# First mixer's output projection as seven half-width products per chunk, with the borrowed ring places filled later

## The chip, the cores and the metric

The kernel runs on one core of a Trainium2 chip. The metric is the device time of one execution in microseconds (us), lower is better; the time before is the median of three runs.

Engines, as the profile names them: PE (TensorE matmul), PEld (its weight load), DVE (VectorE), ACT (ScalarE), POOL (GpSimd), SP (SyncE, which here only issues DMAs; SPq in the rows). Matmuls write PSUM, which has 8 banks of 128 x 512 f32 words.

## The reference, cut to what matters

Two networks run one after the other on 256 tokens of width 1024. The first has two layers, and layer 0 works on two streams: the latent tokens `x` and the context `ctx`, 256 tokens each. Its mixer is `conv_mixers`:

```python
def conv_mixers(u, w_in, conv_a, conv_b, conv_b_bias, ln_g, ln_b, w_out):
    p = u @ w_in
    gate_out, gate_in, val, glu_a, glu_g = jnp.split(p, ...)
    y_a = gate_out * depthwise_conv(gate_in * val, conv_a)          # 512 channels
    z = depthwise_conv(glu_a * jax.nn.sigmoid(glu_g), conv_b) + conv_b_bias
    y_b = jax.nn.silu(layer_norm(z, ln_g, ln_b))                    # 512 channels
    return jnp.concatenate([y_a, y_b], axis=-1) @ w_out             # 1024 x 1024
```

The result of both streams is added to the residual, `h + mod[2] * y`, and then each stream goes through an expert layer: 16 experts, each takes its 32 best tokens, with `w_gate`, `w_up` and `w_down` of 1024 x 1024 (4 MB each in f32). A second mixer (attention and a long convolution) and a second expert layer follow, and then the second network.

## The kernel before, in words

Everything is f32. Activations lie with channels on the 128 partitions. `H` ("hidden" in the rows) is the residual, 2 streams x 8 blocks of 128 channels x 256 tokens; `ab.Y` ("ab_y") holds the mixer's 1024 channels as 8 blocks (0 to 3 are `y_a`, 4 to 7 are `y_b`) of 512 columns, the 256 tokens of one stream and then the other's.

**The weight stream.** All large weights come as one stream of 644 chunks of 1 MB (1024 KB), issued by SP in a fixed order (`sync_program`, the `dma_start` at line 832). A chunk fills a slot; two slots are a place. There are 7 places of the ring's own (`ring` in the rows). For the first half of the first expert layer, two more are borrowed (`M.more_ring[0]`): one made of `ring_filter_freq` and `ring_pads`, one of `ring_z` and `ring_filter`. `Ring.__init__` (from line 718) gives each pair of chunks the place that has waited longest, and `come` says from which pair on the borrowed places take part. The chunk of an earlier pair in the same place must have been used up by PE (`chunk_free`, raised by `ring.free`), and SP waits for that in order: a transfer whose wait isn't over holds up all transfers behind it. Counting pairs of chunks from the first pair of the expert weights as pair 0, `come` is pair 1 here, and SP waits before pair 1 for the last `y_b` block (line 819), since the borrowed room holds mixer data until then. Some pairs go as one transfer of 2 MB, some as two of 1 MB (`transfers`, line 391).

The pairs around the change, in order, with the place that each takes before: output weights `out_ab` 0 and 1 (`ring0`), one modulation pair (`ring1`), `out_ab` 2 and 3 (`ring2`), three modulation pairs (`ring3` to `ring5`), then pair 0 (`ring6`), pairs 1 and 2 (borrowed), pair 3 (`ring0`), 4 (`ring1`), 5 (`ring2`), 6 to 8 (`ring3` to `ring5`), 9 (`ring6`), 10 and 11 (borrowed), 12 (`ring0`) and so on. Pairs 0 to 95 are the expert weights of the first expert layer, pairs 98 to 105 belong to the second mixer.

**The output projection.** `out_ab` c is the 1024 x 256 slice of `w_out` that makes channel blocks 2c and 2c+1. `project_back` (line 1000) makes each block with 8 matmuls of 128 x 128 weights against 512 columns of `ab.Y` (both streams at once) into one bank. The trace counts two instructions for each f32 matmul. DVE's `back` (line 2493) adds each block to `H` with two instructions (line 2498). In the middle of a block PE does `route` (line 968) for the block before: the router's share of that block and four transposes per block for the expert layer's token-major copy (`U2T`). Block 7's `route` follows after the last block; it also sums the squares that ACT (line 2008) and POOL (line 3381) make of every finished block. Then `moe(0)` begins with the first modulation product after it, then the top-32 selection on DVE, and then the expert products, which use the pairs in order.

## Time and profile before

| | us |
|---|---|
| median of 3 runs (2549.83 to 2551.3) | 2550.35 |
| the profiled execution's own time | 2549.89 |
| its span, first to last instruction | 2548.5 |
| PE busy in the span | 2457.0 (96%) |
| DVE busy | 1257.3 (49%) |
| ACT busy | 436.4 (17%) |
| DMA, mean over the span | 280 GB/s |

The profile is of one execution. Its rows give times from the first instruction on. A busy PE is not a PE at its peak, and the shares are means over stages that have different limits: the page's 40 slices show the DMA engines full in some and half idle in others.

### The profile page before, as it was taken

The numbers are of one execution on the slowest core, as the hardware profiler recorded it, in microseconds if no ns is written. First come the engines' busy times: TensorE is split into PE (matmuls) and PEld (weight loads), VectorE is DVE, ScalarE is ACT, GpSimd is POOL, SyncE is SP. The second block draws the span as 40 slices with busy tenths as digits, with TensorE's granted clock in tenths as the row PEclk, the third lists the DMA queues.
The fourth block names the chain that finished last, engine by engine and source line by source line (L and its number), as shares of the span: only waits on it lengthen the run. The fifth ranks groups of instructions, "written<-read, shape, count | busy, mean of one in ns | idle before, by whom it ended". The sixth has DMA issues, their size and how long they took to land.

```text
span 2548.5 us, 29532 instructions
## 1 busy us (share of the span) xinstructions
PE 2457.0 (96%) x12286; PEld 1553.7 (61%) x12286; DVE 1257.3 (49%) x2175; ACT 436.4 (17%) x1099; POOL 179.5 (7%) x126
## 2 busy tenths in 40 slices
PE   9999999889999999987889999999999999999999
PEld 5344443424578753332348857888866875888884
DVE  4981321212176621110117667665776775673775
ACT  2111100101123210000001002541101101560110
POOL 0011000000000000000000011440001003250000
PEclk9999999999999999999999999999999999999999
DMA  9854899999984499999999863415674974423671
GB/s 394 332 231 181 355 425 427 426 428 428 423 345 165 169 377 427 427 427 427 427 421 341 259 222 149 150 67 210 215 227 154 257 227 154 169 106 135 221 225 39
DMA packets 193904, 712.88 MB, mean 280 GB/s; under 512 B 117284, under 2 KB 121892, under 8 KB 128364
## 3 DMA queue, kind: packets, MB, share of 16 engines
q1 hardware_dynamic: 92592, 682.66, 67.2%
q10 hardware_dynamic: 101180, 28.35, 5.3%
q8 instruction: 97, 1.59, 0.3%
q14 instruction: 35, 0.29, 0.0%
HBM read 698.36 MB, written 12.60 MB: 279 GB/s over the span
## 4 chain that ended last, share of the span: by engine, by line
PE 77%; DMA 16%; DVE 5%; ACT 1%; issue 0%; POOL 0%; SPq 0%; DVEq 0%; another core or an unknown queue 0%; POOLq 0%
PE bank L855 75%; DMA ring<-in_stream 8%; DMA ring_high<-in_stream 4%; DMA ring_low<-in_stream 4%; PE bank L858 2%; DVE hidden L2731 1%; DVE ab_z L2561 1%; DMA hidden_turned<-normed 1%; DVE moe_results L2756 0%; DVE small L3300 0%; DVE hidden L3297 0%; DVE small L3303 0%; POOL ab_ln_sum L3426 0%; ACT hidden L2376 0%; DVE ring L3067 0%
## 5 line engine op out<-in xcount | busy, mean ns | idle before, releaser
L855 PE MATMUL bank<-ring,gates 128*128 128x256 f32 (+1 forms) x1760 | 433.6, 391 | 3.5 <-DVE ring L3067 2.4
L855 PE MATMUL bank<-ring,moe_chosen 128*64 128x512 f32 (+1 forms) x2304 | 391.7, 491 | 33.1 <-DMA ring<-in_stream 32.8
L855 PEld LDWEIGHTS bank<-ring,gates 128*128 128x128 f32 x1760 | 333.6, 190 | 71.1 <-issue 23.0
L855 PE MATMUL bank<-ring,normed 128*128 128x256 f32 x1448 | 339.5, 380 | 1.4 <-DMA ring<-in_stream 1.4
L855 PEld LDWEIGHTS bank<-ring,moe_chosen 128*64 128x64 f32 x2304 | 147.8, 137 | 248.9 <-issue 197.1
L855 PEld LDWEIGHTS bank<-ring,normed 128*128 128x128 f32 x1448 | 273.2, 190 | 40.7 <-issue 2.3
L855 PE MATMUL bank<-normed,ring 128*128 128x256 f32 (+2 forms) x1152 | 289.4, 406 | 2.4 <-DVE normed L2542 1.5
L855 PEld LDWEIGHTS bank<-normed,ring 128*128 128x128 f32 x1152 | 189.4, 190 | 98.7 <-issue 84.2
L855 PE MATMUL bank<-ring,ffn_hidden 128*128 128x512 f32 x352 | 170.6, 592 | 0.0
L855 PE MATMUL bank<-ring,moe_turned 128*64 128x512 f32 x576 | 128.8, 595 | 17.5 <-DMA ring<-in_stream 14.3
L2747 DVE TENSOR_TENSOR moe_silu<-bank,moe_silu 128x512 f32<-128x512 f32 x32 | 22.1, 692 | 249.4 <-PE bank L855 249.4
L2756 DVE COPY moe_results<-bank 32x512 f32<-32x512 f32 x36 | 24.8, 690 | 243.1 <-PE bank L855 242.7
L3067 DVE TENSOR_TENSOR ring<-ring,ring 128x1024 f32<-128x1024 f32 x117 | 142.2, 1215 | 1.6
L855 PEld LDWEIGHTS bank<-ring,ffn_hidden 128*128 128x128 f32 x352 | 66.9, 190 | 82.5 <-issue 75.6
L2267 ACT ACTIVATE gates<-gates,small 128x256 f32<-128x256 f32 x88 | 44.4, 508 | 411.6 <-DVE gates L3080 222.2
L855 PEld LDWEIGHTS bank<-ring,moe_turned 128*64 128x64 f32 x576 | 41.1, 137 | 100.9 <-issue 84.3
L2081 ACT COPY moe_results<-bank 32x512 f32<-32x512 f32 x36 | 20.7, 575 | 466.7 <-PE bank L855 466.4
L2561 DVE SCALAR_TENSOR_TENSOR ab_z<-ab_pad_b,vectors,ab_z 128x512 f32<-128x512 f32 x120 | 90.2, 752 | 4.3
L3067 DVE TENSOR_TENSOR ring<-ring 128x1024 f32<-128x1024 f32 x71 | 85.8, 1209 | 0.0
L855 PE MATMUL bank<-ring,hidden 128*128 128x512 f32 x168 | 84.5, 592 | 0.0
L3147 DVE TENSOR_TENSOR ring<-ring 128x512 f32<-128x512 f32 x88 | 62.2, 706 | 38.2 <-PE bank L855 38.2
L3442 POOL TENSOR_TENSOR na_bias<-na_bias,na_mask 128x512 f32<-128x512 f32 x16 | 21.4, 1374 | 782.0 <-PE bank L855 782.0
(448 smaller groups left out, 2720.4 us busy)
## 6 DMA issues: line engine op xcount, KB each, us to landing
ring<-in_stream SPq DMA_DIRECT2D x318, 1024.0 KB, 7.3
ring<-in_stream SPq DMA_DIRECT2D x115, 2048.0 KB, 30.5
ring_low<-in_stream SPq DMA_DIRECT2D x7, 2048.0 KB, 43.7
ring_far<-in_stream SPq DMA_DIRECT2D x7, 2048.0 KB, 45.3
ring_high<-in_stream SPq DMA_DIRECT2D x6, 2048.0 KB, 45.1
hidden_turned<-normed ACTq DMA_DIRECT2D x44, 256.0 KB, 7.3
ffn_hidden<-hidden_turned ACTq DMA_DIRECT2D x44, 256.0 KB, 7.3
hidden<-in_stream SPq DMA_DIRECT2D x9, 1024.0 KB, 31.0
```

The costliest lines, as they stand in the source:

```text
L855: return nc.tensor.matmul(o, lhsT, rhs, start=start, stop=stop, skip_group_check=True)
L858: return nc.tensor.transpose(o, x, ident[0:x.shape[0], 0:x.shape[0]])
L2081: ins = nc.scalar.copy(m.YG[CAP * e:CAP * e + CAP, i, 0:512], bank[4][CAP * i:CAP * i + CAP, :])
L2267: nc.scalar.activation(y.sg[:, t, :], (y.C2 if t else y.C1)[:, 0, :], ACT.Silu, scale=y.rinv_t[:, t:t + 1]).then_inc(*done.up((tag, l, "si ...
L2561: ins = v.scalar_tensor_tensor(out=z_j, in0=ab.PB[:, :, k:k + T], scalar=tap("conv_b", k, j), in1=z_j, op0=ALU.mult, op1=ALU.add)
L2731: v.scalar_tensor_tensor(out=H[:, s, n, :], in0=bank[5 + n % 3][:, T * i:T * i + T], scalar=M.MOD[:, l, 5, n, s:s + 1], in1=H[:, s, n, :], ...
L2747: v.tensor_tensor(m.SG, bank[1][:, :], m.SG, ALU.mult).then_inc(*done.up((tag, "hidden", g, e)))
L2756: ins = v.tensor_copy(m.YG[CAP * e:CAP * e + CAP, i, 512:1024], bank[4][64 + CAP * i:64 + CAP * i + CAP, :])
L3067: v.tensor_tensor(tw[:, i], a, b, ALU.subtract).then_inc(*done.up((tag, l, "t", c, i)))
L3147: v.tensor_tensor(to[:, i], a, b, ALU.subtract).then_inc(*done.up((tag, l, "dt", c, i)))
L3442: nc.gpsimd.tensor_tensor(part, part, mask, ALU.add).then_inc(*done.up(("na_bias", l, t) if h == NA_H - 2 else None))
```

## The change

The four output chunks are each computed with the seven block products of a 2 x 2 scheme in place of eight. For chunk c the weights are cut into four blocks: rows `gated` (k 0 to 3, the `y_a` half) and `normed` (k 4 to 7), columns 2c and 2c+1. The tokens are cut likewise: `gated` and `normed` rows by stream 0 and stream 1. Each product is 4 matmuls of 128 x 128 weights against 256 columns.

- DVE makes, per chunk, four sums of weight blocks (`out_weight_sums`, three of them into new tiles and one over the chunk itself in its ring slot), and once four sums of token blocks (`out_token_sums`, 128 x 1024 each).
- PE's `out_group` runs the seven products into banks 4 (`first`), 2, 5 and 1; `route` for the two blocks of the chunk before stands behind the third and the fourth product; `route` for blocks 6 and 7 both stand behind the last group.
- ACT copies bank 4 into `ab.first`; DVE's `out_sums` puts the products together with four additions and adds the four pieces to `H` (line 2597 in the changed kernel).
- The tiles of sums lie in the room of the two borrowed places. So `come` moves from pair 1 to pair 3, and SP's wait before it is now for `("ab", "back", 7)`, DVE's very last addition of the projection.

```diff
+    four_blocks = lambda name, at, n, width: put(name, arena + 4 * at, n, 4, width)
+    pads, filters = -(-low // 8) * 8, -(-high // 8) * 8
+    here, there = four_blocks("ab_token_sums", filters, 2, T), four_blocks("ab_token_sums_2", pads, 2, T)
+    ab.TS = [here[:, 0], here[:, 1], there[:, 0], there[:, 1]]
...
-BACK_BANKS = {"ab": (4, 5, 1, 2), "cd": (2, 3, 4, 5)}
+AB_OUT_GROUPS = KB // 2
+AB_FIRST_BANK, AB_PRODUCTS = 4, (2, 5, 1)
...
-        come = self.come = [at("expert", 0, 0, 0, 0) + 1, at("expert", 1, 0, 0, 0) + 3]
+        come = self.come = [at("expert", 0, 0, 0, 0) + 3, at("expert", 1, 0, 0, 0) + 3]
...
         if i == 2 * ring.come[0]:
 
-            sp.wait_ge(*S.scalar.at(("y_b", JB - 1)))
+            sp.wait_ge(*S.vector.at(("ab", "back", 2 * AB_OUT_GROUPS - 1)))
...
+        pe.wait_ge(*ring.landed(name))
+        pe.wait_ge(*A.at(("ab", "first", c - 1) if c else ("y_b", JB - 1)))
+        product(first[:, 0:T], block(0, normed), tokens(normed, 0)).then_inc(*done.up(("ab", "first", c)))
+        if c:
+            pe.wait_ge(*V.at(("ab", "z", c - 1)))
+        product(z[:, T:2 * T], weights(0), summed(0))
+        for j in range(0 if c else JB):
+            pe.wait_ge(*V.at(("y_a", j)))
+        product(x[:, 0:T], block(0, gated), tokens(gated, 0))
+        if c:
+            route(0, "ab", 2 * c - 2)
+            pe.wait_ge(*V.at(("ab", "w", c - 1)))
+        product(w[:, T:2 * T], weights(3), tokens(gated, 1))
+        if c:
+            route(0, "ab", 2 * c - 1)
+        product(x[:, T:2 * T], weights(1), summed(1)).then_inc(*done.up(("ab", "x", c)))
+        product(z[:, 0:T], weights(2), summed(2)).then_inc(*done.up(("ab", "z", c)))
+        product(w[:, 0:T], block(1, gated), summed(3)).then_inc(*ring.free(name))
...
-        project_back(0, "ab", "out_ab", ab.Y, 512, (*range(JB, KB), *range(JB)))
+        for c in range(AB_OUT_GROUPS):
+            out_group(c)
+            if c == 1:
+
+                pe.wait_ge(*V.at(("moe0", "shift")))
+                ada_part(1, 1, 0)
+        route(0, "ab", KB - 2)
+        route(0, "ab", KB - 1)
...
         for k in range(KB):
+            if l == 0 and k in (0, 2, 4):
+                for c in range(2) if k == 0 else (k // 2 + 1,):
+                    first(c)
...
+        dve.wait_ge(*TE.at(("ab", "x", c)))
+        dve.wait_ge(*done.now())
+        v.tensor_tensor(two(y0), two(x[:, :]), wide(ab.first, 2), ALU.add).then_inc(*done.up(("ab", "x", c)))
+        dve.wait_ge(*done.now())
+        added(0, 2 * c, y0[:, 0:T]).then_inc(*done.up())
+        dve.wait_ge(*TE.at(("ab", "z", c)))
+        v.tensor_tensor(two(y1), two(z[:, :]), wide(y0[:, T:2 * T], 2), ALU.add).then_inc(*done.up())
+        dve.wait_ge(*done.now())
+        v.tensor_tensor(y0[:, T:2 * T], y1[:, 0:T], z[:, T:2 * T], ALU.add).then_inc(*done.up(("ab", "z", c)))
+        dve.wait_ge(*S.chunk.at(("out_ab", c)))
+        dve.wait_ge(*done.now())
+        v.tensor_tensor(y1, y1, w[:, :], ALU.add).then_inc(*done.up(("ab", "w", c)))
...
         gated(AB_OUT_ORDER[0])
+        out_weight_sums(0)
         invert("ln_root", ab.rinv)
         for j in range(JB):
             v.tensor_tensor(ab.Z[:, j, :], ab.Z[:, j, :], ab.rinv, ALU.mult).then_inc(*done.up(("whitened", j)))
-        for j in AB_OUT_ORDER[1:]:
+        for j in AB_OUT_ORDER[1:-1]:
             gated(j)
+        out_token_sums((0,))
+        gated(AB_OUT_ORDER[-1])
+        out_token_sums((1, 2, 3))
         ada(*AB_PAIRS[len(AB_STEPS) - 1])
         fold(0, 1)
         fold(1, 0)
         dve.wait_ge(*done.now())
         router_weights(0)
-        back("ab", "out_ab", 0, (0, 1))
+        out_weight_sums(1)
+        out_back()
```

SP's transfers from pair 0 on. Before, in the order of issue (128x4096 is a whole pair, 128x2048 one chunk or one piece of a borrowed place):

```order
L832 DMA ring6_55<-in_stream 128x4096
L832 DMA ring_filter_freq_137<-in_stream 128x2048
L832 DMA ring_pads_138<-in_stream 128x2048
L832 DMA ring_z_139<-in_stream 128x2048
L832 DMA ring_filter_140<-in_stream 128x2048
L832 DMA ring0_49<-in_stream 128x4096
L832 DMA ring1_50<-in_stream 128x2048 x2
L832 DMA ring2_51<-in_stream 128x2048 x2
```

The same place in the changed kernel:

```order
L842 DMA ring6_55<-in_stream 128x4096
L842 DMA ring0_49<-in_stream 128x4096
L842 DMA ring1_50<-in_stream 128x4096
L842 DMA ring_filter_freq_137<-in_stream 128x2048
L842 DMA ring_pads_138<-in_stream 128x2048
L842 DMA ring_z_139<-in_stream 128x2048
L842 DMA ring_filter_140<-in_stream 128x2048
L842 DMA ring2_51<-in_stream 128x2048 x2
```

Pairs 1 and 2 now go to `ring0` and `ring1`, which come free when the second output chunk and the modulation pair are used up, and the borrowed places get pairs 3 and 4, ahead of pair 5 in `ring2`.

PE from the start of the projection. Before, to the end of block 2 (`small` is the modulation's condition; `kept` holds the identity and ones):

```order
L855 MATMUL bank4<-ab_y_82,ring0_49 128x512 x8
L855 MATMUL bank5<-ab_y_82,ring0_49 128x512 x5
L855 MATMUL bank3<-moe0_router_91,kept_59 128x32 x8
L858 MATMUL bank6<-kept_59,hidden_56 128x128 x4
L855 MATMUL bank5<-ab_y_82,ring0_49 128x512 x3
L855 MATMUL bank1<-ab_y_82,ring0_49 128x512 x5
L855 MATMUL bank0<-hidden_56,moe0_router_91 32x256 x4
L858 MATMUL bank7<-kept_59,hidden_56 128x128 x4
L855 MATMUL bank1<-ab_y_82,ring0_49 128x512 x3
```

Now, the first group and the first products of the second:

```order
L865 MATMUL bank4<-ab_y_82,ring0_49 128x256 x4
L865 MATMUL bank5<-ab_token_sums_144,ab_weight_sums_146 128x256 x4
L865 MATMUL bank2<-ab_y_82,ring0_49 128x256 x4
L865 MATMUL bank1<-ab_y_82,ab_weight_sums_146 128x256 x4
L865 MATMUL bank2<-ab_token_sums_144,ab_weight_sums_146 128x256 x4
L865 MATMUL bank5<-ab_token_sums_2_145,ring0_49 128x256 x4
L865 MATMUL bank1<-ab_token_sums_2_145,ring0_49 128x256 x4
L865 MATMUL bank4<-ab_y_82,ring0_49 128x256 x4
L865 MATMUL bank5<-ab_token_sums_144,ab_weight_sums_2_147 128x256 x4
L865 MATMUL bank2<-ab_y_82,ring0_49 128x256 x4
L865 MATMUL bank3<-moe0_router_91,kept_59 128x32 x8
```

Two blocks of 8 x 512 columns became 28 x 256 columns, and the first `route` moved from the middle of block 1 to behind the third product of the second group.

DVE behind one chunk. Before, the two blocks of chunk 0 and the copy of the router's shift:

```order
L2498 SCALAR_TENSOR_TENSOR hidden_56<-bank4,modulation_62,hidden_56 128x256 x2
L2498 SCALAR_TENSOR_TENSOR hidden_56<-bank5,modulation_62,hidden_56 128x256 x2
L2504 COPY moe0_shift_92<-bank3 128x32
```

Now, for the same chunk:

```order
L2608 TENSOR_TENSOR ab_sums_149<-bank2,ab_first_148 128x512
L2597 SCALAR_TENSOR_TENSOR hidden_56<-ab_sums_149,modulation_62,hidden_56 128x256
L2612 TENSOR_TENSOR ab_sums_2_150<-bank5,ab_sums_149 128x512
L2614 TENSOR_TENSOR ab_sums_149<-ab_sums_2_150,bank5 128x256
L2617 TENSOR_TENSOR ab_sums_2_150<-ab_sums_2_150,bank1 128x512
L2597 SCALAR_TENSOR_TENSOR hidden_56<-ab_sums_2_150,modulation_62,hidden_56 128x256 x2
L2597 SCALAR_TENSOR_TENSOR hidden_56<-ab_sums_149,modulation_62,hidden_56 128x256
L2584 TENSOR_TENSOR ab_weight_sums_146<-ring2_51 128x512
```

Three of the four pieces of a chunk, for both of its blocks, now reach `H` only after the chunk's seventh product, and the weight sums of the chunk after the next stand between two chunks.

## Rows read from the trace of the kernel before

**Rows 1.** The page: transfer rate in 40 slices of the span (64 us each).
```profile
GB/s 394 332 231 181 355 425 427 426 428 428 423 345 165 169 377 427 427 427 427 427 421 341 259 222 149 150 67 210 215 227 154 257 227 154 169 106 135 221 225 39
```

**Rows 2.** Windows: stretch, length, busy us (x instructions) of each engine, PEclk, DMA share, GB/s.
```profile
195.00:263.00 68.00, 67.79 (x249) 32.24 (x251) 10.50 (x36) 11.47 (x20) 7.62 (x6) 1.00 0.48 184
330.00:437.00 107.00, 104.50 (x516) 43.32 (x514) 26.02 (x58) 12.34 (x24) 0.00 (x0) 1.00 1.01 426
437.00:740.00 303.00, 275.17 (x1725) 136.43 (x1722) 80.05 (x187) 43.15 (x105) 5.08 (x4) 1.00 1.01 425
```

**Rows 3.** Timeline of PE: start, us, what, [idle before it <- what ended it].
```profile
442.85 3.65 PE L855 MATMUL bank<-ring,moe_chosen 128*64 128x512 f32 x16 [1.34 <-DMA ring<-in_stream]
...
728.97 10.63 PE L855 MATMUL bank<-ring,normed 128*128 128x256 f32 x48 [1.42 <-DMA ring<-in_stream]
```

**Rows 4.** Timeline of SP, single issues: start, us, what.
```profile
195.10 0.33 SPq L832 DMA_DIRECT2D ring<-in_stream  x1
...
197.20 0.47 SPq L832 DMA_DIRECT2D ring_filter<-in_stream  x1
...
226.34 0.33 SPq L832 DMA_DIRECT2D ring<-in_stream  x1
...
259.06 0.33 SPq L832 DMA_DIRECT2D ring<-in_stream  x1
...
264.57 0.33 SPq L832 DMA_DIRECT2D ring<-in_stream  x1
...
277.50 0.33 SPq L832 DMA_DIRECT2D ring<-in_stream  x1
...
312.51 0.33 SPq L832 DMA_DIRECT2D ring<-in_stream  x1
```

**Rows 5.** DMA issues in windows of one issue: us to landing, issues at 197.20, 259.06, 312.51, 434.5.
```profile
ring_filter<-in_stream SPq DMA_DIRECT2D x1, 1024.0 KB, 15.5
...
ring<-in_stream SPq DMA_DIRECT2D x1, 1024.0 KB, 4.8
...
ring<-in_stream SPq DMA_DIRECT2D x1, 2048.0 KB, 16.7
...
ring_filter_freq<-in_stream SPq DMA_DIRECT2D x1, 1024.0 KB, 35.2
```

**Rows 6.** Timeline of PE, the projection and what follows.
```profile
194.91 11.32 PE L855 MATMUL bank<-ab_y,ring 128*128 128x512 f32 x26
...
226.24 1.92 PE L855 MATMUL bank<-ring,small 128*32 128x512 f32 x16
...
258.86 0.95 PE L855 MATMUL bank<-kept,ab_sigmoid 128*128 128x1 f32 x8
...
262.58 1.92 PE L855 MATMUL bank<-ring,small 128*32 128x512 f32 x16
```

**Rows 7.** Windows of PE alone: 16 matmul instructions of 512 columns, and 16 of 256.
```profile
240.96:247.83 6.87, 6.87 (x18) 1.00 0.41 150
771.83:775.29 3.46, 3.46 (x18) 1.00 0.83 348
```

**Rows 8.** Groups by line: busy us, mean ns of one | idle before.
```profile
L855 PEld LDWEIGHTS bank<-ring,normed 128*128 128x128 f32 x1448 | 273.2, 190 | 40.7 <-issue 2.3 <-DMA ring<-in_stream 1.9 <-DVE normed L3022 0.6
L3067 DVE TENSOR_TENSOR ring<-ring,ring 128x1024 f32<-128x1024 f32 x117 | 142.2, 1215 | 1.6
```

**Rows 9.** Timeline of DVE before and in the projection.
```profile
182.10 3.35 DVE L2439 RECIPROCAL ab_rinv<-ab_rinv 128x512 f32<-128x512 f32 x1 [5.35 <-ACT ab_rinv L1885]
...
195.11 0.69 DVE L2598 TENSOR_TENSOR ab_y<-ab_y,bank 128x512 f32<-128x512 f32 x1 [5.93 <-PE bank L855]
...
197.16 0.28 DVE L2630 TENSOR_TENSOR moe_router<-vectors,modulation 128x128 f32<-128x128 f32 x1
...
259.06 0.88 DVE L2498 SCALAR_TENSOR_TENSOR hidden<-bank,modulation,hidden 128x256 f32<-128x256 f32 x2 [6.43 <-PE bank L855]
```

**Rows 10.** Timeline of POOL, the sum of the squares of block 6.
```profile
253.38 1.27 POOL L3381 TENSOR_TENSOR ab_sigmoid<-ab_sigmoid,ab_squares 128x512 f32<-128x512 f32 x1 [6.75 <-ACT ab_squares L2008]
```

More of the change, by code:

```diff
@@ new lines, in out_token_sums @@
+    def out_token_sums(which):
+        ab = M.ab
+        tokens = lambda ks, s: ab.Y[:, ks, T * s:T * s + T]
+        gated, normed = slice(0, JB), slice(JB, KB)
+        terms = ((tokens(normed, 1), tokens(normed, 0)), (tokens(gated, 1), ab.TS[0]), (tokens(gated, 1), tokens(normed, 1)), (tokens(gated, 0), ab.TS[1]))
+        for i in which:
+            dve.wait_ge(*(done.now() if i else A.at(("y_b", JB - 1))))
+            v.tensor_tensor(ab.TS[i], *terms[i], ALU.subtract).then_inc(*done.up(("ab", "t", i)))
@@ L2506, in mixer_ab, with out_back @@
+    def out_back():
+        for c in range(AB_OUT_GROUPS):
+            if c == 1:
+                dve.wait_ge(*TE.at(("moe0", "shift")))
+                v.tensor_copy(M.moe[0].shift, bank[SHIFT_BANK[0]][:, 0:NS * NE]).then_inc(*done.up(("moe0", "shift")))
+            out_sums(c)
+            if c + 2 < AB_OUT_GROUPS:
+                out_weight_sums(c + 2)
     def mixer_ab():
```

61 lines of the change are left out of this document (55 added, 6 removed).

## The prediction

> **What bounds the kernel now.** Read the rate of the DMA engines over the whole span first [rows 1]. From the sixth slice to the eleventh (319 to 701 us) it stands near 426 GB/s, and nowhere above 428: that is the stream of expert weights. In slices 3 and 4, around the change, it falls to 231 and 181, and in 13 and 14, the second mixer, to 165 and 169. Then read the stretches around the change [rows 2]: in the output projection (195 to 263) PE is busy and the DMA engines are at 0.48; from 330 to 437 both are full, at 426 GB/s; from 437 to 740 the DMA engines are full and PE has 28 us of gaps. The gaps end on landings: I show the one at 442.85 (pair 40), and the last, for the second mixer's first weights, at 728.97 [rows 3]. So PE is ahead of the stream up to 437, and from there to 729 it does each piece when it lands. What PE gains before 437 is only a longer wait after it. The end of the kernel is moved by what moves the landings, and those are gated by when SP can issue.
>
> The issues say where the stream has holes [rows 4]. Pairs 0 to 2 go out from 195.10 on; pair 3 at 226.34, when `out_ab` 1 is used up; the second half of pair 5 at 259.06, pair 6 at 264.57. Between them the queue runs dry. Pair 17 is issued at 312.51 and lands 16.7 us later, at 329.2 [rows 5]; from there to pair 102 one transfer follows the other. I take the landing of pair 17 as the gauge: what the change does to it, it does to the end.
>
> **The change on PE.** A block of 16 instructions with 512 columns takes 6.87 us, a product's 8 with 256 columns half of 3.46, 1.73 us; the granted clock is 1.00 (2.4 GHz) in both [rows 7]. The second is measured in the other mixer, with the same shape and the same kind of sums, so I take it as it is. Eight blocks are 55.0 us, 28 products 48.4: 6.6 us less. The projection now runs from 194.91 to 258.86 [rows 6]: 63.95 us, of which 55.0 are blocks, 1.9 the modulation part, 7.1 seven `route` calls. One that has transposes alone (for block 6) moves behind the last product; I estimate it at 0.4, below the mean of 1.0, as it lacks the router's part. The last product then ends at 194.91 + 48.4 + 1.9 + 6.7 = 251.9, if nothing waits.
>
> Does something wait? The first product needs the last `y_b`. That is what SP waits for between pairs 0 and 1, and as the issues of 195.10 and 197.20 stand 2.1 us apart with three others between them [rows 4], it was over by then. The third needs the last gated block, at 195.80 [rows 9], and comes at 194.9 + 2 x 1.73 = 198.4. The first chunk's weight sums, four additions of 512 elements at half of the 1.22 us that 1024 take [rows 8], some 2.5 us, fall into the 5.35 us in which DVE waits for the root [rows 9]. The first token sum falls into the 5.93 us before 195.11. The other three are 1.22 us each [rows 8]: 195.80 to 199.4; the fifth product, the first that needs one, comes at 201.8. Then come what stood there before (195.80 to 197.4, 1.7 us) and the second chunk's weight sums (2.5): DVE is free at 203.7, and the fifth product, for which it waits next, ends at 203.8. PE's next need is bank 5 at 194.91 + 8 x 1.73 = 208.75; DVE has it free 0.7 + 0.4 us behind the sixth product (205.5), at 206.7. Slack 2.0 us here, and more in later groups, where DVE has some 6 us of work in 14. So no wait, at cost nothing; were DVE later by more than 2.0, PE would be later by the rest.
>
> **The change behind the last product.** Before, DVE starts 0.2 us behind the last matmul and needs 0.88 [rows 6, 9]. Now it adds bank 1 (0.69) and then three pieces (0.88 + 0.45): 251.9 + 0.2 + 0.7 + 1.3 = 254.1. That is the wait of SP before pair 3. PE's own tail: block 6 is on `H` only at 253.2, ACT squares it (0.6), POOL needs 1.27 [rows 10], and the sum of squares that began at 258.86 now begins at 255.1. What followed it took 3.7 us up to 262.58 [rows 6]. The expert layer starts on PE at about 258.8, 3.8 us earlier.
>
> **The change on the stream.** Queued behind SP's waiting instruction are pairs 3, 4 and all after them. Pairs 1 and 2 wait for `out_ab` 1 and the modulation pair, used up at about 222 (194.9, 14 products, the first two `route` calls) and 224, and are there by 237; PE, which is done with pair 0 near 273.7, wants them after that. At 254.1 pairs 3, 4 and 5 go out in one burst, as all they wait for is over; pair 6 joins at about 260.8 (before 264.57, less 3.8), pairs 7 and 8 within 4 us, pair 9 when pair 0 is used, near 273.7 (277.50 before [rows 4]), when pairs 6 to 8 are still to come. From there each pair is issued 3.8 us earlier than before, while its turn comes later, so I see no hole.
>
> A pair is 2.097 MB; at 426 GB/s [rows 2] that is 4.92 us. The start of a burst costs more: pairs 0 to 2 were issued from 195.10, the last piece landed at 197.20 + 15.5 = 212.7 [rows 4, 5], so 17.6 for 14.8, a surcharge of 2.8. Pair 17 is the fifteenth from pair 3: 254.1 + 2.8 + 15 x 4.92 = 330.7. Before 329.2. The change of the end is +1.5 us. The saving of the seven products is in it: without it SP would be released at 260.7 and the sum would be +8.1. Put otherwise, the later filling of two pairs costs 9.8 us of stream and gets back what the earlier end and the holes of before (12 pairs from 264.57 to 329.2 are 64.6 us, 59.0 of them transfer) leave.
>
> Bounds. From below, the chain ends 0.5 us sooner and the surcharge is that of a lone chunk: 4.8 to landing [rows 5], 2.46 of it transfer, so 2.3: +0.5. From above, the holes that pairs 6 to 17 have beyond a surcharge, 64.6 - 59.0 - 2.8 = 2.8, come again: +4.3. I take +1.5, since the queue is deeper in every place where those holes were.
>
> Later the ring's places are shifted too: the borrowed places leave at pair 48 having held pairs 39 and 40, not 46 and 47, so pairs 48 to 54 wait for pairs 41 to 47, two further than before. That is 9.8 us of lead, of 35.2 at pair 46 [rows 5]; 25 are left. Pairs 99 and 100 also wait for two later ones, with over 20 us of lead left. Cost nothing, covered by the queue.
>
> The profiled execution took 2549.89 with a span of 2548.5; the same sum gives 2551.4. The median of the runs shown is 2550.35, 0.46 above it, so 2551.9.
>
> **A rule against it.** A window of 16 matmul instructions with 256 columns holds 16 weight loads of 190 ns [rows 7, 8] and takes 16 x 216: the loads lie under the matmuls. The Trainium skill, "TensorE: Matmul & The Clock Gate", section "The mechanism", says that a weight load overlaps a running matmul only when it goes to another row group of the array, and these all use all rows. By that rule loads would be exposed. Here the trace disagrees, with 216 ns an instruction. A rival below holds what it would cost.
>
> **Rivals.**
> - PE sets the end after all, and its earlier start is kept: -3.8 us, 2546.5; were the tail hidden as well, the whole 6.6, 2543.7. For it: PE is 96% busy. Against: 28 us of gaps between 437 and 740, ended by landings [rows 2, 3]. 0.08, a half of it with the whole 6.6.
> - DVE holds PE between groups, and it ends slower. The place is bank 5 before the second product of group 1, the point a DVE lateness of 2.0 us. All of these sums read every other half row of a tile. If they ran at half speed, 3.7 + 2.5 = 6.2 us more, less 2.0, PE and SP's release come 4.2 later: +5.7, 2556.1. For it: DVE goes without a pause from 195 to 207. Against: additions of ring halves cut the same way take 1.22 for 1024 [rows 8]. 0.15.
> - The weight loads are not covered at 256 columns: 96 more loads of 190 ns, +18.2 on the projection and so on SP's release: +19.7, 2570. The page above would have it so. Against: rows 7. 0.02.
>
> **How the numbers follow.** Forecast 0.75, its own range +0.5 to +4.3, 2550.9 to 2554.7. About 0.2% (5.1 us) is what a measurement of this kernel can tell from no change. Faster than that: the half of the first rival and a little for what I overlook, 0.05. Slower: most of the second, the third, and a thin end of the forecast (holes and a little lateness together), 0.17. The rest, 0.78, within. For 8 in 10 the range goes from 2547, short of the first rival's value, to 2557, past the second's.
>
> **What would show it.** In the profile after: products of 1.73 us, the last one ending near 252; SP's issue into `ring_filter_freq` at about 254 (before 195.5); the DMA engines idle between 235 and 256 and then full with no gap; pair 17 landing near 330.7; PE's first wait for a landing before 437, its gaps up to 740 some 4 to 6 us larger; the first weights of the second mixer at about 730.4 (before 728.9). I am wrong if pair 17 lands before 329 or after 334, if PE waits for DVE in groups 1 to 3, or if the shift at 729 is not the one at pair 17.

## The result

The kernel after takes 2554.70 us (median of 20 runs), the kernel before beside it 2551.29 (20 runs). By the medians that is 3.4 us slower. The ratio of the runs is 1.0018, 95% interval 1.0012 to 1.0024, so 4.6 us with 3.1 and 6.1 as its bounds: it goes with the means, and a few long runs of the kernel after (up to 2566.31) lift its mean to 2555.94. The profiled execution took 2553.35 with a span of 2552.0, 3.46 more than that of before. The prediction said 2551.9, with 0.78 for a change within 0.2% (it is, narrowly), 2550.9 to 2554.7 for the mechanism that it named (the median is at the upper end), and +1.5 us where +3.4 came. So the mechanism has to be shown, and the 1.9 us that it was short be found.

**The projection.** The timeline of PE in the kernel after (start, us, what, idle time before it and what ended it), in the place of [rows 6] and [rows 7]:

```profile
207.45 1.89 PE L865 MATMUL bank<-ab_y,ring 128*128 128x256 f32 x8
209.18 1.89 PE L865 MATMUL bank<-ab_token_sums,ab_weight_sums 128*128 128x256 f32 x8
...
248.84 3.62 PE L865 MATMUL bank<-ab_token_sums,ring 128*128 128x256 f32 x16
253.76 0.66 PE L868 MATMUL bank<-kept,hidden 128*128 128x128 f32 x4 [1.30 <-DVE hidden L2597]
255.77 1.05 PE L865 MATMUL bank<-kept,ab_sigmoid 128*128 128x1 f32 x8 [1.35 <-POOL ab_sigmoid L3514]
256.75 0.78 PE L865 MATMUL bank<-hidden,moe_router 128*32 128x256 f32 x8
257.45 1.87 PE L865 MATMUL bank<-kept,ab_squares 128*128 128x1 f32 x8
...
261.06 3.33 PE L865 MATMUL bank<-ring,small 128*32 128x512 f32 x16
```

From one product's start to the next it is 1.73 us (207.45 to 209.18), as reckoned, and the last ends at 248.84 + 3.62 = 252.5. The first starts at 195.37 and not at 194.91, which is 0.46 of the 0.6 between 252.5 and the 251.9 of the prediction. Windows of the kernel after show that PE never waits for DVE within the groups: 67.60 - 64.95 = 2.65 us of gaps in the first row are the 1.30 and the 1.35 above. And they show what I had not thought of, in the last column but two, the granted clock:

```profile
core 0: us, PE busy (x) PEld busy (x) DVE busy (x) ACT busy (x) POOL busy (x), PEclk, DMA share, GB/s
195.40:263.00 67.60, 64.95 (x353) 52.44 (x355) 33.71 (x71) 13.61 (x26) 8.17 (x6) 0.96 0.35 137
235.00:254.00 19.00, 17.70 (x92) 14.72 (x91) 8.02 (x15) 2.75 (x6) 2.54 (x2) 1.00 0.00 1
252.00:256.00 4.00, 1.35 (x9) 0.70 (x8) 2.24 (x5) 2.25 (x3) 1.27 (x1) 1.00 0.16 31
256.00:258.00 2.00, 2.00 (x19) 1.44 (x18) 0.00 (x0) 1.29 (x5) 0.00 (x0) 0.78 0.93 340
258.00:260.00 2.00, 2.00 (x11) 2.00 (x11) 0.18 (x1) 1.05 (x3) 0.00 (x0) 0.50 0.99 418
...
262.00:264.00 2.00, 2.00 (x16) 0.31 (x8) 0.30 (x2) 0.09 (x1) 0.00 (x0) 0.51 1.00 422
264.00:266.00 2.00, 2.00 (x22) 0.57 (x22) 1.18 (x4) 0.00 (x0) 0.00 (x0) 1.00 1.03 426
330.00:437.00 107.00, 102.95 (x506) 42.46 (x504) 26.02 (x58) 12.32 (x24) 0.00 (x0) 1.00 1.01 425
437.00:740.00 303.00, 273.81 (x1715) 134.02 (x1712) 76.67 (x184) 42.94 (x103) 5.08 (x4) 1.00 1.01 426
```

After the two gaps the clock falls to 0.50 (1.2 GHz) until about 264. The modulation part that took 1.92 us in [rows 6] takes 3.33. So TensorE begins that part 1.5 us earlier than before, not 3.8, and by its end it has only 0.1 us left of its gain.

**The stream.** Single issues of SP in the kernel after, for [rows 4]: pair 0, pair 3, the second half of pair 5, pair 6, pair 9, pair 17.

```profile
195.56 0.33 SPq L842 DMA_DIRECT2D ring<-in_stream  x1
...
254.52 0.33 SPq L842 DMA_DIRECT2D ring_filter_freq<-in_stream  x1
...
257.30 0.47 SPq L842 DMA_DIRECT2D ring<-in_stream  x1
...
264.46 0.33 SPq L842 DMA_DIRECT2D ring<-in_stream  x1
...
277.38 0.33 SPq L842 DMA_DIRECT2D ring<-in_stream  x1
...
312.39 0.33 SPq L842 DMA_DIRECT2D ring<-in_stream  x1
```

The times to landing of the second half of pair 5 and of pair 17 in the kernel after, the latter for the 16.7 of [rows 5]:

```profile
ring<-in_stream SPq DMA_DIRECT2D x1, 1024.0 KB, 15.7
...
ring<-in_stream SPq DMA_DIRECT2D x1, 2048.0 KB, 20.1
```

Pair 17 lands at 312.39 + 20.1 = 332.5, before at 329.2. The same shift stands 400 us later at the first weights of the second mixer. This is PE's row there, before at 728.97 [rows 3]:

```profile
732.42 10.63 PE L865 MATMUL bank<-ring,normed 128*128 128x256 f32 x48 [1.41 <-DMA ring<-in_stream]
```

It is 3.45 us later, and the span is 3.5 us longer. Between these two executions, nothing is won or lost from pair 17 to the end.

### The profile page after: what moved, and what is told of

It reads as the page before. It is cut to its first block, busy times and chain, and to the rows that moved or that the text cites. A ratio compares the mean times of both kernels' runs of the same rounds, so it can differ in the third digit from the quotient of the medians.

```text
span 2552.0 us, 29776 instructions
## 1 busy us (share of the span) xinstructions
PE 2455.0 (96%) x12382; PEld 1573.1 (62%) x12382; DVE 1285.0 (50%) x2211; ACT 437.2 (17%) x1103; POOL 180.8 (7%) x126
## 4 chain that ended last, share of the span: by engine, by line
PE 77%; DMA 17%; DVE 4%; ACT 1%; issue 0%; POOL 0%; SPq 0%; another core or an unknown queue 0%; DVEq 0%; POOLq 0%
PE bank L865 75%; DMA ring<-in_stream 9%; DMA ring_high<-in_stream 4%; DMA ring_low<-in_stream 3%; PE bank L868 2%; DVE hidden L2864 1%; DVE ab_z L2689 1%; DMA hidden_turned<-normed 1%; DVE moe_results L2889 0%; SPq L842 0%; POOL ab_ln_sum L3559 0%; DVE ring L3200 0%; DVE cd_y L2502 0%; DVE moe_turned L2885 0%; DVE small L3433 0%
## 5 line engine op out<-in xcount | busy, mean ns | idle before, releaser
L865 PE MATMUL bank<-ring,moe_chosen 128*64 128x512 f32 (+1 forms) x2352 | 400.8, 491 | 30.5 <-DMA ring<-in_stream 30.5
L865 PEld LDWEIGHTS bank<-ring,normed 128*128 128x128 f32 x1448 | 273.0, 190 | 42.3 <-issue 3.1
```

What stands on the lines that cost most here:

```text
L865: return nc.tensor.matmul(o, lhsT, rhs, start=start, stop=stop, skip_group_check=True)
```

## The experiments

All of them against the kernel before, which ran beside them (median 2551.60 in the first four, 2552.06 in the next four, 2551.79 in the last three). The gauge columns come from each profiled execution as they did above, one for each kernel. The medians of before differ by up to 0.8 us from one group of experiments to the next, so a difference of less than about 1 us between the medians of two groups tells nothing.

```
kernel                 pair 3 asked  pair 17 lands  2nd mixer on PE  span    median   ratio (95%)
before                 226.34 (own)  329.2          728.97           2548.5  2551.29
after                  254.52        332.5          732.42           2552.0  2554.70  1.0018 (1.0012-1.0024)
ring_only              260.59        338.4          738.21           2558.2  2559.51  1.0035 (1.0022-1.0048)
tail_warm              254.67        332.8          732.65           2551.3  2553.70  1.0012 (1.0003-1.0021)
early_release          253.67        332.1          731.94           2551.5  2552.80  1.0004 (0.9995-1.0013)
parts_moved            in own place  333.5          733.37           2556.2  2556.98  1.0021 (1.0012-1.0030)
sums_later             254.14        332.4          732.27           2554.5  2554.42  1.0009 (1.0000-1.0018)
light_before                                        703.10           2523.2  2525.22  0.9896 (0.9882-0.9909)
light_after                                         704.08           2524.3  2524.91  0.9894 (0.9880-0.9907)
light_warm                                          699.88           2520.3  2521.20  0.9879 (0.9865-0.9892)
part_alone             in own place  331.9          731.69           2551.5  2552.37  1.0001 (0.9992-1.0009)
before_part                          330.6          730.35           2550.8  2552.53  1.0003 (0.9994-1.0012)
one_part               in own place  327.3          727.66           2547.6  2549.81  0.9989 (0.9980-0.9998)
```

**ring_only: the ring part without the new projection.**

```diff
--- before
-        come = self.come = [at("expert", 0, 0, 0, 0) + 1, ...
+        come = self.come = [at("expert", 0, 0, 0, 0) + 3, ...
-            sp.wait_ge(*S.scalar.at(("y_b", JB - 1)))
+            sp.wait_ge(*S.vector.at(("ab", "back", KB - 1)))
```

> The kernel before with its old output projection, and of the change only the ring part: the borrowed places are filled from pair 3 on instead of pair 1, behind the last addition of the old projection. In the kernel after, pair 3 was asked for at 254.5 us and pair 17 landed 3.3 us later than in the kernel before. Theory (the stream decides: the time is what the last landings make it, and they move with the request of pair 3): the old projection's last addition ends near 260, so the request moves some 5.5 us later than in the kernel after, pair 17 lands at about 338 (329.2 before, 332.5 after), and the run is 7 to 9 us slower than before. Rival (TensorE decides: its own start into the expert layer sets the end): the old projection ends as it did, so the time stays within 1 us of before.

Measured: 2559.51, 7.9 us over before. SP's issue of pair 3 and the time to landing of pair 17, in the trace of this kernel:

```profile
260.59 0.33 SPq L832 DMA_DIRECT2D ring_filter_freq<-in_stream  x1
...
313.13 0.33 SPq L832 DMA_DIRECT2D ring<-in_stream  x1
```

```profile
ring<-in_stream SPq DMA_DIRECT2D x1, 2048.0 KB, 25.3
```

The request of pair 3 is 6.07 us later than in the kernel after, and pair 17 lands 5.9 us later (338.4): one for one. The second mixer follows by 5.8 and the span by 6.2; between the medians it is 4.8. The whole change thus splits. The later filling costs 9.2 us at pair 17, the shorter projection gives 5.9 back.

**tail_warm: TensorE kept busy in the two gaps.**

```diff
--- after
+        def hold_clock(n):
+            for i in range(n):
+                mm(bank[AB_FIRST_BANK][:, 0:T], ones, M.kept[:, 0:T], True, True)
+
+        pe.wait_ge(*A.at(("ab", "first", AB_OUT_GROUPS - 1)))
+        hold_clock(3)
         route(0, "ab", KB - 2)
+        hold_clock(4)
         route(0, "ab", KB - 1)
```

> The kernel after with seven more 128x256 products whose sums nobody reads, three ahead of the routing of block 6 and four ahead of that of block 7, in the two gaps of 1.30 and 1.35 us in which TensorE waited. Both theories: the granted clock stays at 1.0 between 256 and 266 us, where it was 0.50 from 257 to 264, and TensorE comes into the expert layer at about 258, 3 us earlier. Theory (the stream decides): the request of pair 3 is VectorE's and does not move, so the landing of pair 17 moves by less than 1 us and the median by 0.5 us at most. Rival (the lost clock is what ate the gain): 2 to 3 us faster than the kernel after, so at or below the kernel before.

Windows of this kernel show a clock that stays, and its timeline of PE the modulation parts (one, and then two in one row) at full speed again, 1.6 and 3.0 us earlier than in the kernel after (261.06 and 264.64):

```profile
256.00:258.00 2.00, 2.00 (x22) 1.55 (x20) 0.00 (x0) 1.30 (x5) 0.00 (x0) 1.00 0.85 299
258.00:260.00 2.00, 2.00 (x22) 1.53 (x25) 0.86 (x5) 1.89 (x4) 0.00 (x0) 1.00 1.05 442
...
262.00:264.00 2.00, 2.00 (x24) 0.65 (x20) 1.86 (x7) 0.00 (x0) 0.00 (x0) 1.00 1.07 442
```

```profile
259.50 1.92 PE L865 MATMUL bank<-ring,small 128*32 128x512 f32 x16
...
261.68 3.64 PE L865 MATMUL bank<-ring,small 128*32 128x512 f32 x32
```

Pair 17 lands at 332.8 and the second mixer begins at 732.65, 0.2 later than in the kernel after: three microseconds of TensorE changed nothing there. The median is 1.0 below that of the kernel after, more than the 0.5 that I allowed; the two ratios' intervals overlap (1.0003 to 1.0021 and 1.0012 to 1.0024). The trace has no such gain before 732; in the profiled execution 0.9 us arise behind it (2551.3 - 732.65 = 1818.7, against 1819.6 in the kernel after), where the edit changes nothing. I count the rival's 2 to 3 us as refuted by the landings and the 1.0 as open.

**early_release: pair 3 released by TensorE's last product.**

```diff
--- after
-    ab.first = put("ab_first", arena + 4 * (end1 + TT * 2 * T + 3 * 4 * P), T)
+    ab.first = put("ab_first", arena + 4 * (high + SLOT), T)
-            sp.wait_ge(*S.vector.at(("ab", "back", 2 * AB_OUT_GROUPS - 1)))
+            sp.wait_ge(*S.chunk.at(("out_ab", AB_OUT_GROUPS - 1)))
-        y0, y1 = ab.both
+        y0, y1 = (ab.both if c < AB_OUT_GROUPS - 1 else (ab.Y[:, JB - 1, :], ab.both[1]))
```

> The kernel after, with the last group's intermediate sums put outside the borrowed ring places, so that the transfer of pair 3 waits for the last read of the output weights by TensorE's products and not for VectorE's last additions. The request of pair 3 moves from 254.5 to about 252.3. Theory (the stream decides): the landing of pair 17 moves from 332.5 to about 330.5 and the run is 1.5 to 2.5 us faster than the kernel after, slightly above the kernel before. Rival (the stream is held by the ring places of pairs 6 to 17, which TensorE's clock and start set): no more than 0.3 us.

Measured: 2552.80, 1.9 below the kernel after. In the profiled execution the projection began 1.2 us later than in that of the kernel after (pair 0 asked at 196.74), so the request of pair 3 must be read from there: 253.67 - 196.74 = 56.9 us, against 254.52 - 195.56 = 59.0. It is 2.0 earlier, and pair 17, read the same way, 1.6.

**parts_moved: all of the second modulation's pairs ahead.**

```diff
--- after
         if c == 1:
-            ada_quarter(1, 1, 0)
-    for q in range(1, KB // 2):
-        ada_quarter(1, 1, q)
+            for q in range(KB // 2):
+                ada_quarter(1, 1, q)
...
-        come = self.come = [at("expert", 0, 0, 0, 0) + 3, ...
+        come = self.come = [at("expert", 0, 0, 0, 0) + 6, ...
...
-                ada_part(1, 1, 0)
+                for q in range(KB // 2):
+                    ada_part(1, 1, q)
...
-        modulation = (lambda q: ada_part(1, 1, q + 1)) if l == 0 else ...
+        modulation = (lambda q: kept_warm(4)) if l == 0 else ...
```

> The kernel after, with all four pairs of the second layer's modulation streamed and multiplied ahead of the last projection chunks (between chunk 1 and chunk 2) and none between the routing and the first experts; the borrowed places are then filled from the third expert pair on as before, counted from the new order. TensorE gets 5.8 us of work earlier and loses it behind the projection, and the three ring places of those pairs come free some 20 to 30 us earlier. Theory (the stream decides, and it stood idle between 236 and 254 us for want of places): about half of that idle time is filled, and the run is 2 to 7 us faster than the kernel after. Rival (the stream's idle time is only moved, since the projection's end and with it the borrowed places' release comes 5.8 us later): within 1.5 us of the kernel after, or slower by up to 3.

Measured: 2556.98, 2.3 slower than the kernel after. The theory's number was wrong, the rival's right (up to 3 slower). At pair 17 only 1.0 of it is seen (333.5), and 0.7 of that is a later start, so the step from pair 9 to the 2.3 is not shown; where the profiled execution loses more stands at the end of the section on the prediction. Windows of this kernel show where the stream stands still now:

```profile
278.00:282.00 4.00, 4.00 (x32) 3.27 (x32) 1.37 (x6) 1.50 (x4) 0.00 (x0) 1.00 0.00 0
282.00:286.00 4.00, 4.00 (x25) 2.08 (x22) 0.39 (x2) 0.00 (x0) 0.00 (x0) 1.00 0.41 152
```

Three more pairs land by 252, but pair 9 needs a place that the use of pair 0 frees, and TensorE, 5.5 us later, comes to that at 282.9 (277.4 after). The queue has run dry by 278.7. I had looked at the places before the borrowed ones alone. A single pair more, in place of three, is tried in part_alone and one_part.

**sums_later: VectorE's sums away from GpSimd's.** The four sums of the first chunk move behind the first token sum.

```diff
--- after
         gated(AB_OUT_ORDER[0])
-        out_weight_sums(0)
         invert("ln_root", ab.rinv)
...
         out_token_sums((0,))
+        out_weight_sums(0)
```

> The kernel after with the first chunk's four weight sums moved on VectorE from ahead of the reciprocal at 182.5 us to behind the token sum at 189.6 us, where VectorE has 4.7 us of idle time; they no longer run beside GpSimd's three additions at 175.6 us. Theory (the two engines slow each other, and GpSimd's additions hold TensorE's product of ones): those three additions take 4.4 us instead of 4.93, each sum takes 0.7 us instead of up to 1.75, the projection starts 0.4 to 0.5 us earlier, and the run is about 0.5 us faster, which the interval can hardly tell. Rival (the 0.5 us are a scatter from run to run): the additions stay at 4.9 us.

The sums and GpSimd's additions, first in the trace of the kernel after:

```profile
176.60 1.16 DVE L2584 TENSOR_TENSOR ab_weight_sums<-ring 128x512 f32<-128x512 f32 x1
177.79 1.64 DVE L2584 TENSOR_TENSOR ab_weight_sums<-ab_weight_sums,ring 128x512 f32<-128x512 f32 x1
179.36 1.75 DVE L2584 TENSOR_TENSOR ring<-ring 128x512 f32<-128x512 f32 x1
181.03 0.68 DVE L2584 TENSOR_TENSOR ab_weight_sums<-ring,ab_weight_sums 128x512 f32<-128x512 f32 x1
```

```profile
175.62 4.93 POOL L3559 TENSOR_TENSOR ab_ln_sum<-ab_ln_sum,ab_squares 128x512 f32<-128x512 f32 x3 [8.49 <-ACT ab_squares L2041]
```

and then with the sums later:

```profile
190.39 0.68 DVE L2584 TENSOR_TENSOR ab_weight_sums<-ring 128x512 f32<-128x512 f32 x1
191.11 0.69 DVE L2584 TENSOR_TENSOR ab_weight_sums<-ab_weight_sums,ring 128x512 f32<-128x512 f32 x1
```

```profile
175.77 4.41 POOL L3559 TENSOR_TENSOR ab_ln_sum<-ab_ln_sum,ab_squares 128x512 f32<-128x512 f32 x3 [8.50 <-ACT ab_squares L2041]
```

Apart, the additions take 4.41 and each sum 0.68; beside each other 4.93 and up to 1.75. The product of ones behind them comes 0.4 us earlier (at 180.32, before at 180.70) and with it the projection. The Trainium skill, "SBUF — State Buffer", section "Who interferes with whom", says that a DVE instruction with both inputs in SBUF contends with a GpSimd instruction that reads SBUF; the trace agrees in that, with the numbers above. Of VectorE's two-port modes it also says that whoever issues first has the shared ports for the whole instruction and the other is blocked. Here, with additions that both read two tiles of SBUF, both are longer while they overlap (4.93 for 4.41 on one side, 1.16 + 1.64 + 1.75 for 3 x 0.68 on the other), so over a string of instructions each engine loses some time. The median, 0.3 below that of the kernel after, can't tell 0.5 from nothing.

**light_before and light_after: the stream out of the way.** In both, the transfers of the first expert layer are halved from pair 6 on.

```diff
+            if name[:2] == ("expert", 0) and i // 2 >= ring.come[0] + 3:      # + 5 on the kernel before
+                to, src = to[:, 0:SLOT * chunks // 2], src[:, 0:SLOT * chunks // 2]
             nc.sync.dma_start(to, src).then_inc(*ring.arrival(i).up(i if last else None))
```

> The kernel before, but from pair 6 of the first expert layer on only the first half of each transfer's columns is fetched (that layer's weights are stale beyond it, so the output is another one); every wait stays. It is the base for the next run. The stream should stop bounding the first expert layer: the expert layer of 460 us becomes shorter by what TensorE waited for, so 20 to 100 us in all.

> The kernel after with the same halved transfers. Read against the kernel before with halved transfers, not against the full ones. Theory (with full transfers the change costs what the late request of pair 3 costs the stream; TensorE itself comes to pair 0 only 0.1 us earlier, as its gain in the projection is lost to the halved clock): with the stream out of the way the 3.3 us are gone and the two differ by 0.5 us at most, either way. Rival (the change loses time on TensorE or VectorE as well, in the expert layer): after remains 2 us or more slower. A second rival (the projection's gain of some 4 us is real and only hidden by the stream): after is 3 us or more faster.

Windows, first of light_before, then of light_after. The stream is at 236 to 245 GB/s, and PE is busy for 248 of 253 us where it was busy for 227 to 229 with full transfers:

```profile
437.00:690.00 253.00, 247.99 (x1536) 119.15 (x1534) 60.70 (x144) 32.51 (x77) 3.79 (x3) 1.00 0.71 245
```

```profile
437.00:690.00 253.00, 247.99 (x1524) 118.44 (x1522) 60.11 (x142) 32.16 (x76) 3.79 (x3) 1.00 0.69 236
```

Before and after take 2525.22 and 2524.91 (4 runs each): the 3.4 us are gone. What was lost was lost in the stream, and TensorE brings nothing of the projection's 6.6 us with it, as expected from the 0.1 us above. (In the profiled executions light_after is 1.1 us longer; its projection began 1.6 us later, pair 0 being asked for at 196.56 and 194.98. The section on the prediction shows that most of these 1.6 come from near 20 us, where the edit has no part.)

**light_warm: the same with the clock held.** The edit of tail_warm on light_after.

> The kernel after with the halved transfers and with the seven products that hold the clock in the two gaps ahead of routing 6 and routing 7. Read against the kernel after with halved transfers (2524.91 us). Theory (the halved clock between 257 and 264 us costs TensorE 3 us, and this shows in the time as soon as the stream does not set it): TensorE comes to pair 0 at about 275 instead of 278, and the run is 2 to 3.5 us faster. Rival (something else than TensorE and the stream sets the expert layer, VectorE's or ScalarE's part in it): no more than 0.7 us.

PE comes to pair 0 at 272.18 (276.37 in light_after, 275.40 in light_before), to the second mixer at 699.88 (704.08, 703.10); the 275 and 278 of the expectation were both too late. The first of these rows, in light_after and then in light_warm:

```profile
276.37 3.65 PE L867 MATMUL bank<-ring,moe_chosen 128*64 128x512 f32 x16
```

```profile
272.18 3.65 PE L867 MATMUL bank<-ring,moe_chosen 128*64 128x512 f32 x16
```

The median is 3.7 us below light_after, just above the range of 2 to 3.5, and 4.0 below light_before. In the two profiled executions PE moves by 4.2, of which 1.1 lies in the start of the projection (pair 0 asked at 195.45 and 196.56) and 3.1 in the clock. With the stream out of the way, the clock's 3 us show in the time; this is the very edit that moved no landing with full transfers.

**part_alone and before_part: one modulation pair more ahead, on either kernel.**

```diff
         if c == 1:
             ada_quarter(1, 1, 0)
-    for q in range(1, KB // 2):
+            ada_quarter(1, 1, 1)
+    for q in range(2, KB // 2):
...
-        come = self.come = [at("expert", 0, 0, 0, 0) + 3, ...      # on before: + 1
+        come = self.come = [at("expert", 0, 0, 0, 0) + 4, ...      # on before: + 0
...
                 ada_part(1, 1, 0)
+                ada_part(1, 1, 1)
...
-        modulation = (lambda q: ada_part(1, 1, q + 1)) if l == 0 else ...
+        modulation = (lambda q: ada_part(1, 1, q + 1) if q else kept_warm(2)) if l == 0 else ...
```

> The kernel after with one edit: two modulation pairs instead of one behind chunk 1, so that four expert pairs fit ahead of the borrowed places. No products that hold the clock, no early release, the weight sums as in the kernel after. The four edits together made 4.9 us. Theory (the extra pair's transfer of about 5 us falls into the stream's idle time and 1.9 us of it are paid back, since TensorE and with it the release of the borrowed places comes 1.9 us later): 2.5 to 4 us faster than the kernel after, within 1 us of the kernel before; pair 17 lands at about 329.3. Rival (without the held clock the use of pair 0 comes too late for pair 9, as where all four were moved): less than 1 us faster than the kernel after.

> The kernel before with the same one edit: two modulation pairs instead of one behind chunk 1. The borrowed places are asked for behind the extra pair as early as before, near 195 us, by the first expert pair now. Theory (before has no backlog of transfers behind the old projection: pair 6 waits for a ring place that TensorE frees at 264.5 us and the queue is empty then, so TensorE's 1.9 us earlier work only delays it): no gain; pair 17 lands at 329 to 331 and the run is 0 to 2 us slower than before. Rival (an extra pair in the stream's idle time is worth 3 us in either kernel, so the faster version above owes nothing to the change): 2 to 4 us faster than before.

(`kept_warm(n)` makes n products that nobody reads.)

part_alone: 2552.37, 2.3 below the kernel after, just under the range. The gauge does not bear this out: pair 17 lands at 315.27 + 16.6 = 331.9, not at 329.3, so 0.6 earlier than in the kernel after, or 1.3 with the start taken out, which is 0.7 later (pair 0 asked at 196.22); its borrowed places are asked for at 256.90, and the clock is at 0.50 from 260 to 268 in its windows. before_part: 2552.53, 0.7 above before, pair 17 at 330.6, 1.4 later than in before. The rival is refuted. The stream does not stand on a backlog here: in before it moves 133 GB/s from 256 to 264, and windows of before_part show it waiting for places, with a clock that falls here too (0.50 from 264 to 266):

```profile
266.00:268.00 2.00, 2.00 (x16) 0.71 (x19) 1.11 (x5) 0.10 (x1) 0.00 (x0) 0.78 0.65 279
268.00:270.00 2.00, 2.00 (x24) 0.60 (x20) 1.86 (x7) 0.00 (x0) 0.00 (x0) 1.00 0.06 16
```

So the extra pair gained at the gauge in the kernel after, where six pairs are asked for between 254.5 and 268.8, and not in the kernel before. That the backlog makes the difference fits these rows; no run varies it by itself, and the fallen clock of before_part may have a part in its 1.4.

**one_part: the four edits together.** early_release, tail_warm, sums_later and part_alone on the kernel after.

> The kernel after with four edits together: the products that hold the clock in the two gaps, the early release of the borrowed places, the weight sums later, and of the second layer's modulation one pair more (two instead of one) streamed and multiplied behind chunk 1, so that four expert pairs instead of three fit into the ring before the borrowed places, which are filled from pair 4. TensorE does 1.9 us of work earlier, and of the filler behind the routing half remains in its place. Theory (the stream decides): the extra pair lands in the time in which the stream stood idle, the remaining ones follow from the release at about 253.5 us, the landing of pair 17 comes at 326 to 328 (332.5 after, 329.2 before), and the run is 4.5 to 6.5 us faster than the kernel after and 1.5 to 3.5 us faster than before. Rival (moving all four pairs cost 2.3 us, since TensorE's use of pair 0 and so the request of pair 9 came later): 0 to 2 us slower than before.

Measured: 2549.81 against 2552.06, ratio 0.9989 (0.9980 to 0.9998): 2.2 us faster than before and 4.9 below the median of the kernel after. Pair 17 lands at 311.16 + 16.1 = 327.3, as reckoned. The row of the second mixer is

```profile
727.66 10.63 PE L866 MATMUL bank<-ring,normed 128*128 128x256 f32 x48 [1.42 <-DMA ring<-in_stream]
```

1.3 us earlier than in the kernel before. The single edits made 1.9, 1.0, 0.3 and 2.3 in the medians, in sum 5.5. At the gauge they do not add up like that. From the request of pair 0 to the landing of pair 17 it is 136.9 us in the kernel after, 1.6 less in early_release and 1.3 less in part_alone, 0.2 and 0.3 more in tail_warm and sums_later, but 4.7 less with all four. So the edits help each other. Together with the extra pair the held clock may count: pair 9, which needs the place of pair 0, is asked for at 280.25 in part_alone and at 276.14 here. No run has just these two edits, so this is not shown. This is the version that beats both kernels, by little.

## Why the prediction was right in kind and short in size

**What bounds the kernel: right.** That what TensorE gains before 437 only lengthens a wait, and that the landing of pair 17 is the gauge, is shown from three sides. In ring_only the request of pair 3 comes 6.1 us later than in the kernel after, and its landings and its second mixer follow one for one. tail_warm moves TensorE by 3 us and the landings stay. light_after against light_before loses the difference when the stream is out of the way. Over all ten kernels with full transfers, the second mixer begins 399.7 to 400.4 us after pair 17 has landed.

**The products, their weight loads, DVE between the groups: right.** 1.73 us each, no wait within the groups. The second and third rivals fell with this.

**The release of pair 3: right, 254.52 for 254.1.** All of the difference is the start of the projection, 0.46 later. A later start of the projection was nowhere in the sum. The step that let the first chunk's weight sums "fall into the 5.35 us in which DVE waits for the root" placed them where they cost DVE nothing and did not ask who else uses the memory then. The traces of all thirteen kernels say how much that is. In the five where the granted clock is below 1.00 between 18 and 22 us (0.67 to 0.77: ring_only, early_release, parts_moved, part_alone, light_after) pair 0 is asked for at 195.72 to 196.74. In the eight where it stays at 1.00, it is at 195.45 to 195.71 with the sums beside GpSimd's additions and at 194.98 to 195.18 without. So the sums cost the 0.5 us, and most of the rest of the scatter is a fall of the clock 170 us earlier, which kernels alike up to there have or have not (light_after and after).

**The sum for the stream: a term mis-sized.** "254.1 + 2.8 + 15 x 4.92 = 330.7" should have been 332.5. In the kernel after, the second half of pair 5 lands at 257.30 + 15.7 = 273.0. Pairs 3 to 5, 14.8 us of transfer, so take 18.5 from 254.52, a surcharge of 3.7 and not 2.8; that is 0.9. Pairs 6 to 17 take 59.5 us, 4.96 each and not 4.92: 0.5. The start makes 0.4. Together 1.8. The surcharge had been read from one burst, pairs 0 to 2, and taken for every burst; the burst of pairs 3 to 5 has 3.6 in ring_only too (263.33 + 15.6 - 260.59 = 18.3). The upper bound, +4.3, did hold it.

**TensorE's tail: wrong, without a price.** "The expert layer starts on PE at about 258.8, 3.8 us earlier" was 261.06, and 0.1 us earlier by the end of that part. The step had both waits in its sum (the second over at 255.1, measured 255.77) and left out that the granted clock falls behind them: what it took as 3.7 us, from the sum of squares to the modulation part, takes 5.3 (255.77 to 261.06). The Trainium skill, "TensorE: Matmul & The Clock Gate", section "HAM oscillation — how this bites in real kernels", describes such a fall for a kernel that waits for a transfer behind each short stretch of matmuls; here two waits of 1.3 us for other engines, with 0.66 us of work between them, were followed by 7 us at 0.50. It cost nothing only since the stream decided; light_warm shows its price, 3 us.

**The first rival,** that PE's earlier start is kept, -3.8, would have failed in two ways: the start was not earlier, and had it been, the landings would not have followed.

**What would show it.** I had said I would be wrong if pair 17 landed before 329 or after 334 (332.5), if PE waited for DVE in the groups (no), or if the shift at 729 were not that of pair 17 (3.45 and 3.3). PE's first wait for a landing is at 431 now (442 before), as named. Its gaps between 330 and 740 grew by 2.9 us, less than the 4 to 6 named: the 3.8 us that PE was to be earlier did not come, and of what I named only the later landings remain.

**Behind the second mixer's start.** The spans of parts_moved and sums_later are longer than their shift at the second mixer explains (2556.2 - 733.37 = 1822.8 and 1822.2, against 1819.6 in before and after). The traces show where most of it lies. This is one modulation part behind the second mixer, in the kernel after and in sums_later:

```profile
913.42 2.80 PE L865 MATMUL bank<-ring,small 128*32 128x256 f32 x48
```

```profile
913.39 4.30 PE L865 MATMUL bank<-ring,small 128*32 128x256 f32 x48
```

The granted clock in sums_later is 0.57 from 913 to 917, in the kernel after 1.00. In parts_moved it falls at the same part (4.29 for 2.80) and once more at 1446, where 8 instructions of 256 columns take 3.42 for 1.97. That is 2.9 of its 3.2 us, and 1.5 of the 2.6 of sums_later. Whether the edits have a part in these falls no run shows. The other 1.1 us of sums_later and the 1.0 us of tail_warm are open.

## What to carry to other kernels

Where a stream of transfers decides, as here, reckon an edit in the engines only up to the moment at which it changes when a transfer can be asked for, and carry that moment to one landing behind the next full stretch of the queue; in all ten kernels here the second mixer began 399.7 to 400.4 us after it. Work taken off the engine that is not late is worth what it releases, and before a pair is moved ahead in the ring, look whether there is a backlog behind it and whether the next place comes free before that is gone (parts_moved lost by the second, before_part did not gain). After a rearrangement that shortens a dense stretch, look for new waits of about a microsecond at its end and for the granted clock right behind them. And before a difference of one or two microseconds between two executions is put down to an edit, compare the granted clock of both over the whole span: a single fall made 1.5 us here.

## What the hardware showed that I had not expected

- Two gaps of 1.30 and 1.35 us on TensorE brought the granted clock from 1.00 to 0.50 (1.2 GHz) for about 7 us; fourteen matmul instructions of 256 columns in the gaps kept it at 1.00. It fell for about 7 to 10 us in the six profiled executions that have these gaps, and not in tail_warm and light_warm. In one_part, with the same fourteen, it fell all the same for a shorter time, at 260 to 264, without such gaps. Many small matmul instructions stand ahead of the fall; that they are its cause is not shown:

```profile
258.00:260.00 2.00, 2.00 (x23) 1.57 (x22) 0.00 (x0) 1.20 (x5) 0.00 (x0) 1.00 1.02 434
260.00:262.00 2.00, 2.00 (x10) 1.31 (x9) 1.47 (x7) 1.99 (x3) 0.00 (x0) 0.65 0.99 418
262.00:264.00 2.00, 1.88 (x11) 0.53 (x14) 1.19 (x5) 0.01 (x1) 0.00 (x0) 0.50 1.03 434
```

- VectorE additions of 0.68 us took up to 1.75 us beside GpSimd additions, and three of the latter 4.93 instead of 4.41.
- The clock also fell in places where no edit was: between 18 and 22 us in five of the thirteen profiled executions, at 913 in two. Work that TensorE did there without waiting took 1.5 us longer (2.80 and 4.30 for the same 48 instructions).
